# Inverse roots as exp(-ln/2) on ScalarE, and the last expert job's rows added on chip, in a one-core two-layer decoder trunk

## What is computed

```python
def rmsnorm(x, g):
    y = x32 * lax.rsqrt(jnp.mean(x32 * x32, axis=-1, keepdims=True) + EPS)
    return y * g
def moe_ffn(h, w_router, b_router, wg, wu, wd):
    logits = jnp.einsum('btd,de->bte', h, w_router) + b_router
    probs = jax.nn.softmax(logits, axis=-1)
    top_p, top_i = lax.top_k(probs, TOP_K)          # 2 of 8
    top_p = top_p / jnp.sum(top_p, axis=-1, keepdims=True)
    gates = jnp.sum(jax.nn.one_hot(top_i, N_EXPERTS) * top_p[..., None], axis=-2)
    y = 0
    for e in range(N_EXPERTS):
        y = y + gates[..., e:e + 1] * swiglu(h, wg[e], wu[e], wd[e])
    return y
# per layer (the same for both kinds):
    x = x + rmsnorm(mix, g_post_mix)                # mix: conv or attention, and memory attention
    h = rmsnorm(x, g_pre_ffn)
    x = x + rmsnorm(f, g_post_ffn)                  # f: dense SwiGLU (2816) or moe_ffn (8 x 1408)
```

## Time and profile before

| | |
|---|---|
| median of three runs | 1848.36 us (1845.27 to 1849.92) |
| profiled execution, its own time | 1845.7 us |
| its span | 1843.5 us |
| mean granted TensorE clock | 0.952 |
| TensorE matmul busy | 1675.3 us (91%) |
| VectorE, ScalarE, GpSimd busy | 955.3, 738.1, 533.9 us |
| DMA, mean over the span | 153 GB/s |

### The profile page before, as it was taken

How to read it: one execution, slowest core, us unless ns; L and a number is a source line. 1 busy time by engine, 2 the same in 40 slices (tenths; PEclk the granted TensorE clock), 3 DMA queues, 4 the chain that set the end, 5 groups by cost and what they waited for, 6 DMA issues and landing times.

```text
span 1843.5 us, 28946 instructions
## 1 busy us (share of the span) xinstructions
PE 1675.3 (91%) x11254; PEld 1522.8 (83%) x11254; DVE 955.3 (52%) x1145; ACT 738.1 (40%) x964; POOL 533.9 (29%) x326
## 2 busy tenths in 40 slices
PE   6898787899999997899898998899999999999991
PEld 5898677899999997899666586888898988989891
DVE  6796534211111002322486514877686776868764
ACT  6354443222222122221355222554454554545443
POOL 1001222255555343132000020252332524325242
PEclk8899888999999998899898999999999999999996
DMA  6623202144445332021533415399798796987934
GB/s 202 123 90 123 69 23 69 46 142 142 142 142 174 101 131 92 23 92 61 193 126 87 143 58 137 137 284 279 212 269 231 228 270 212 283 217 237 262 126 156
DMA packets 345379, 282.65 MB, mean 153 GB/s; under 512 B 9585, under 2 KB 309661, under 8 KB 345175
## 3 DMA queue, kind: packets, MB, share of 16 engines
q1 hardware_dynamic: 325619, 253.45, 46.9%
q10 hardware_dynamic: 16532, 16.57, 2.6%
q0 software_dynamic: 3168, 11.80, 2.2%
HBM read 247.40 MB, written 35.10 MB: 153 GB/s over the span
## 4 chain that ended last, share of the span: by engine, by line
PE 44%; issue 25%; DVE 12%; POOL 11%; ACT 4%; DMA 1%; SPq 1%; POOLq 0%; ACTq 0%; DVEq 0%
PE ps L2191 34%; POOL ea L841 9%; DVE cT L1518 2%; PE ps L2319 2%; POOL ea L843 1%; DVE wlo L1395 1%; PE ps L2153 1%; DVE rstd L1360 1%; PE ps L2143 1%; PE ps L2216 1%; DVE zc L1837 1%; PE ps L2329 1%; PE ps L2560 1%; PE ps L2509 1%; ACT zc L1166 1%
## 5 line engine op out<-in xcount | busy, mean ns | idle before, releaser
L2720 PE MATMUL ps<-ejx,ewh 128*128 128x384 f32 x1408 | 405.0, 361 | 8.6 <-DVE esg L2049 3.4
L2013 DVE TENSOR_TENSOR ewl<-eraw,ewh 128x2048 fp32r<-128x2048 f32 (+1 forms) x144 | 303.9, 2112 | 161.4 <-ACT ewh L1273 161.0
L1273 ACT ACTIVATE ewh<-eraw 128x2048 fp32r<-128x2048 f32 (+1 forms) x144 | 255.2, 1773 | 278.1 <-PE ps L2723 156.8
L2723 PE MATMUL ps<-ejx,ewl 128*128 128x192 f32 x1408 | 353.9, 251 | 0.0
L2191 PE MATMUL ps<-hh,whi 128*128 128x260 f32 x1504 | 316.7, 293 | 39.0 <-DVE hl L1751 27.5
L2191 PE MATMUL ps<-hl,whi 128*128 128x260 f32 x1504 | 309.3, 288 | 0.0
L2191 PE MATMUL ps<-hh,wlo 128*128 128x260 f32 x1504 | 309.1, 288 | 0.0
L841 POOL TENSOR_TENSOR ea<-eat,ea 128x128 fp32r<-128x128 f32 x88 | 180.3, 2049 | 381.0 <-ACT ea L1308 381.0
L2191 PEld LDWEIGHTS ps<-hh,whi 128*128 128x128 f32 x1504 | 241.0, 195 | 43.2 <-issue 30.0
L2720 PEld LDWEIGHTS ps<-ejx,ewh 128*128 128x128 f32 x1408 | 266.0, 189 | 12.6 <-issue 8.8
L2723 PEld LDWEIGHTS ps<-ejx,ewl 128*128 128x128 f32 x1408 | 270.8, 192 | 0.0
(11 more groups left out here) (401 smaller groups left out, 2619.2 us busy)
## 6 DMA issues: line engine op xcount, KB each, us to landing
eraw<-in_w_gate_e SPq DMA_DIRECT2D x88, 512.0 KB, 4.7
eraw<-in_w_up_e SPq DMA_DIRECT2D x88, 512.0 KB, 6.1
eraw<-in_w_down_e SPq DMA_DIRECT2D x64, 512.0 KB, 6.4
eraw<-in_w_down_e SPq DMA_DIRECT2D x48, 256.0 KB, 2.7
xs<-zero ACTq DMA_DIRECT2D x10, 1152.0 KB, 4.8
raw<-in_w_gate_d SPq DMA_DIRECT2D x22, 512.0 KB, 3.9
raw<-in_w_up_d SPq DMA_DIRECT2D x22, 512.0 KB, 5.1
raw<-in_w_down_d SPq DMA_DIRECT2D x16, 512.0 KB, 4.3
```

Source lines behind the costliest of these rows:

```text
L1273: e.activation(ewh[:, s, 0:n], eraw[:, u % RAW, 0:n], ACT.Copy).then_inc(ew_hi, 1)
L2013: e.tensor_tensor(ewl[:, s, 0:n], eraw[:, u % RAW, 0:n], ewh[:, s, 0:n].bitcast(F32), ALU.subtract)\
L2720: e.matmul(ps[:, q, 0:2 * C], ewh[:, s, o:o + P], ejx[:, k, :, :].rearrange("p h n -> p (h n)"), start=(k == 0), stop=(k == KD - 1), skip_ ...
L2723: ins = e.matmul(ps[:, q, C:2 * C], ewl[:, s, o:o + P], ejx[:, k, 0, :], start=False, stop=(k == KD - 1), skip_group_check=True)
```

## The change

It has two parts.

**Inverse roots.** At roots 1 to 5, at the layer norm and at the router's small norm, ScalarE's root becomes a logarithm and a second ScalarE instruction exp(-0.5 ln) on the same tile; VectorE's reciprocals (128 x 520, and a small one) go. The function tables are preloaded as one set that holds both, in place of the root's.

```diff
-                e.activation(halves(rstd[:, :]), ps[:, 4:6, 0:HALF], ACT.Sqrt, scale=1.0 / D, bias=eps[:, :])\
+                e.activation(halves(rstd[:, :]), ps[:, 4:6, 0:HALF], ACT.Ln, scale=1.0 / D, bias=eps[:, :])\
                  .then_inc(root_ready, 1)
+                e.wait_ge(root_ready, n + 1)
+                e.activation(rstd[:, :], rstd[:, :], ACT.Exp, scale=-0.5).then_inc(rstd_ready, 1)
...
-            e.preload_act_table(ACT.Sqrt)
+            e.preload_act_table_set("natural_log_exp_and_others")
...
             def inverse(n):
 
-                e.wait_ge(root_ready, n + 1)
-                e.reciprocal(rstd[:, :], rstd[:, :]).then_inc(rstd_ready, 1)
                 e.wait_ge(rstd_ready, n)
 
```

```diff
-            with e.Fori(0, nj) as j:
+            def row_back(i, s):
+
+                n = P if i < NT else B
+                e.indirect_dma_start(out=(fo[i][0:n, :], fs1[i][0:n, :])[s], out_offset=None, in_=ys,
+                                     in_offset=bass.IndirectOffsetOnAxis(ap=sle[0:n, s, i:i + 1], axis=0))\
+                 .then_inc(yr_in[i], 16)
...
+            for m in range(KE):
+                if m == 3:
+                    e.wait_ge(er_done, nj * 4)
+                    e.wait_ge(ys_out, nj * 32 + 16)
+                    e.wait_ge(xs_in, 160)
+                    e.wait_ge(last_ready, 1)
+                if m == KE - 1:
+                    e.wait_ge(eg_done, nj * (2 * KE))
+                rest(last, m)
+                if 3 <= m <= 6:
+                    row_back(m - 3, 0)
+                    row_back(m - 3, 1)
+            row_back(NT, 0)
+            row_back(NT, 1)
...
+            def early_sum(i):
+
+                n = P if i < NT else B
+                e.wait_ge(f_act, FA[f"one{i}"])
+                e.scalar_tensor_tensor(out=fo[i][0:n, :], in0=fs1[i][0:n, :], scalar=gme[0:n, 1, i:i + 1],
+                                       in1=fo[i][0:n, :], op0=ALU.mult, op1=ALU.add).then_inc(f_dve, 1)
+
+            def early_lo(i):
+
+                n = P if i < NT else B
+                e.wait_ge(f_act, FA[f"hi{i}"])
+                e.tensor_tensor(flo[i][0:n, :], fo[i][0:n, :], fhi[i][0:n, :].bitcast(F32),
+                                ALU.subtract).then_inc(f_dve, 1)
...
+                if part >= 6:
+                    for i in ((0, 1), (2, 3), (4,))[part - 6]:
+                        n = P if i < NT else B
+                        e.tensor_scalar(ohm[0:n, i, :], colf[0:n, 0:P], own_last[0:n, i:i + 1], None, ALU.is_equal)
+                        for h in range(2):
+                            ins = e.tensor_scalar(ohd[i][0:n, CB * h:CB * h + CB], colf[0:n, P:C], own_last[0:n, i:i + 1], None,
+                                                  ALU.is_equal)
+                if part == 8:
+                    ins.then_inc(last_ready, 1)
...
+                    if u == 9 or u == 10:
+                        early_one(u - 9)
+                    if u == KE:
+                        selection(last)
+                        early_one(2)
+                        e.preload_act_table(ACT.Sqrt)
                     if u == KE + 1:
-                        for c in range(4):
-                            rows_hi(c, j * 4 + (4 + c + 1))
+                        early_one(3)
+                    if u == KE + 2 or u == KE + 3:
+                        early_hi(2 * (u - KE - 2))
+                        early_hi(2 * (u - KE - 2) + 1)
+                    if u == KE + 4:
+                        early_one(4)
...
+            def add_rows(i, part):
+
+                n = P if i < NT else B
+                b = F_BANKS[i]
+                for k in range(4):
+                    c, h = k // 2, k % 2
+                    if i == 0:
+                        if part == 0:
+                            e.wait_ge(f_act, FA[f"y{k}"])
+                        else:
+                            e.wait_ge(f_dve, FD[f"y{k}"])
+                    ins = e.matmul(ps[0:n, b + h, :], sel[:, c, i * P:i * P + n], (eyh, eyl)[part][:, c, 512 * h:512 * h + 512],
+                                   start=False, stop=(part == 1 and c == 1), skip_group_check=True)
+                return ins
+
+            open_tile(0)
+            open_tile(1)
+            add_rows(0, 0)
+            add_rows(1, 0)
+            add_rows(0, 1).then_inc(f_pe, 1)
+            add_rows(1, 1).then_inc(f_pe, 1)
+            for i in range(2, NF):
+                if i == NT:
+                    e.wait_ge(f_dve, FD["w0"])
+                open_tile(i)
+                add_rows(i, 0)
+                add_rows(i, 1).then_inc(f_pe, 1)
```

Further edits: the tail goes through the tiles of 128 rows first and the tile of 8 rows last; in job 0 `result_rows`, `zero_rows` and the store are dropped, and `load_rows(2)` moves from step 7 to step 12; the last job's store of the job before moves from step 10 to step 9:

```diff
-                if u == 7:
+                if u == 12:
                     e.wait_ge(er_done, 4)
                     e.wait_ge(xs_in, 160)
                     load_rows(2)
-                if u == 10:
-                    e.wait_ge(ey_ready, 4)
-                    store_rows(0)
+            e.sem_inc(ys_out, 32)
...
+                    if u == 1 and first:
+                        e.sem_inc(ey_low, 2)
+                        e.sem_inc(ey_ready, 4)
+                    elif u == 1:
                         result_rows(j + 1, j * 32 + 16, j * 2 + 2)
-                    if u == KE + 1:
+                    if u == KE + 1 and not last:
                         for c in range(4):
                             rows_lo(c, j * 4 + (4 + c + 1))
...
-            with e.Fori(0, nj) as j:
+            def selection(j):
+
+                e.wait_ge(last_ready, 2)
+                for c in range(4):
+                    q = EB[eb_at(2 * KE + c)[0]]
+                    eb_wait(j, 2 * KE + c)
+                    if c == 3:
+                        for h in range(2):
+                            for i in range(NT + 1):
+                                n = P if i < NT else B
+                                e.matmul(ps[:, q, 256 + h:257 + h], (ohm[0:n, i, :], ohd[i][0:n, :])[h], gate_last[0:n, i:i + 1],
+                                         start=(i == 0), stop=(i == NT), skip_group_check=True)
+                    for i in ((0, 1, 2), (3, 4))[c % 2]:
+                        n = P if i < NT else B
+                        o = P * (i % 3)
+                        ins = e.transpose(ps[:, q, o:o + n], (ohm[0:n, i, :], ohd[i][0:n, :])[c // 2], ident[0:n, 0:n])
+                    ins.then_inc(er_done, 1)
```

More of the change, by code:

```diff
@@ L2054, in expert_dve @@
+            def expert_dve(j, first=False, last=False):
                 for u in range(PER_JOB):
@@ L2624, in _ @@
                           tmp[0:E, 0, i * P:i * P + (P if i < NT else B)]) for i in range(NT + 1)])
-            def zero_rows(c):
-                for h in range(2):
-                    ins = e.matmul(ps[:, 2 + c, 256 * h:256 * h + 256], ones[:, :], zero[:, 0:256], start=True, stop=True)
-                return ins
-            for c in range(3):
-                zero_rows(c)
             copied_out(e, TP_XT + 8)
```

304 lines of the change are left out of this document (197 added, 107 removed).

## The result

The changed kernel takes 1824.92 us (median of 4 runs, 1821.79 to 1827.86), the kernel before 1846.82 (4 runs, 1844.79 to 1849.92): a ratio of 0.9877, 95% interval 0.9861 to 0.9894. It is faster by 22 us where 36.7 were forecast, and its median lies 0.9 us above the upper end of the range (1824). The profiled execution took 1821.79 us, its span is 1820.0 against 1843.5.

A forecast was written before the change was run, and what follows sets the result against it. TensorE's matmuls fill 91% of the span, so only its waits can be won; -13.4 - 2.5 - 6.0 - 15.7 + 0.8 + 0.1 = -36.7 us gives 1809.0 profiled, 1811.7 median; 8-in-10 range 1801 to 1824.

The forecast's parts named there:

- Inverse roots: Roots 1 to 5 and layer norm: first multiplication starts 2.8 us earlier without the reciprocal; 13.4 us won in sum.
- GpSimd's turn at roots 1 and 3: GpSimd's low part is let in between VectorE's multiplications, so each of these roots wins only 1.3 us.
- TensorE's clock: Behind roots 2, 4 and 5 the shorter wait may keep the clock from falling: 2.5 us won, between 0 and 7.8.
- one of three possible places: Roots 2, 4 and 5 could each lose 2.6 us of work to low clock; the forecast took 2.5 in all.
- Job 0: First expert job: waits for VectorE, low clock behind and a late weight in job 1 go; 6.0 us won.
- The end: After the last job's matmuls: tail with small reciprocals for five tiles, ending at 1827.8; 15.7 us won.
- The last job: Added groups, scalings and gathers nearly fit into idle time; with the selection and its copies, 0.8 us lost.
- a step over is paid by the weights prepared ahead: Last job: where VectorE's added groups, about 0.3 to 1.1 us each, overrun a step, weights prepared ahead cover it.
- 2.8 us "by count": Last job's selection: 10 transposes and 10 matmuls of one column, in place of sixteen transposes of 1.95 us together.
- The gathers: Rival, last job: GpSimd falls behind through gathers beside VectorE's subtraction, TensorE stands 5 us: 1816.7; chance 0.20.
- The written-out job: Rival, last job: instructions run once may arrive later than a loop's; at twice the pace 1889.4; chance 0.04.

The follow-up runs named there:

- a_only: The kernel before with the inverse roots alone changed (logarithm and exponential): 1835.80 us, ratio 0.9937.
- gates_wait: Changed kernel; in the last job ScalarE's first scaling of gathered rows waits for VectorE's gates, no longer for the last one-hot: 1819.69 us, ratio 0.9855.
- spread: gates_wait with down steps between the selection's parts and ScalarE's first two scalings behind the selection's first copies: 1818.62 us, ratio 0.9845; last job 79.4.
- half_gathers: Changed kernel without the four second gathers of 128 rows, the first row added twice: 1828.50 us (one run); last job 88.3.
- warm_router: Changed kernel with six of the eight matmuls of zero rows put back before the router's last waits: 1826.53 us, ratio 0.9881.
- best: late_high and spread together: 1809.80 us, ratio 0.9790 to the kernel before.
- best_down: best with TensorE's wait for all low parts of the dense hidden tiles moved to the down projection's third weight chunk: 1802.74 us, ratio 0.9744.
- best_warm: best with all eight matmuls of zero rows put back: 1806.33 us, ratio 0.9778.
- best_all: best_down with the eight matmuls of zero rows back as in best_warm: 1800.07 us, ratio 0.9746.
- b_only: Changed kernel with root and reciprocal back at all places, so without the new inverse roots: 1840.56 us, ratio 0.9963.
- late_high: gates_wait with ScalarE's next weight tile at roots 1 and 3 moved behind the eight tiles of x: 1811.99 us, ratio 0.9816.

## Why the prediction was wrong

By its own steps:

- **Inverse roots**, -13.4 forecast. 2.8 for each root whose scaling waits alone, 2.4 at the layer norm and 1.3 at root 1 came out as 2.8, 2.4 and 1.1; root 3 gave 1.7. The working held, GpSimd's turn at roots 1 and 3 included.
- **TensorE's clock**, -2.5. The shorter wait saved about 0.9 us of low clock at root 2 (1.7 lost behind it in place of 2.6), and what the stages hold over the 2.8 of the wait itself (2.7 with the router's small root) gives 0.8 at root 4 and, in a_only, 0.7 at root 5: 2.4 in all. That this comes so near to a term that I took as one of three possible places is luck: it was saved in parts at all three. What the term left out is the clock elsewhere: 2.6 us in the dense layer behind a wait that was the same as before, and 1.4 in the router, of which 0.8 to 1.2 come from matmuls that the change removed and that I had costed at nothing. I named them only as work of VectorE, and did not ask what kept the clock up there.
- **Job 0**, -6.0: -6.3. The 0.9 counted as job 1's lies ahead of its first matmul, in the stage of job 0.
- **The end**, -15.7: -15.6. In its parts the first reciprocal came 0.4 us later than forecast, the five tiles took the 13.3 forecast, and the last store 2.2 in place of 2.5.
- **The last job**, +0.8: +11.2. This is the step that failed, at the words "a step over is paid by the weights prepared ahead". I compared the added operations of each engine with that engine's idle time, and asked of waits only whether GpSimd would be late. The change adds a wait of ScalarE for VectorE's last one-hot ahead of a weight that VectorE needs. It costs 3.5 us by itself (gates_wait); 1.4 is the wait that is left there, which went when spread moved the two scalings and split the selection together; and 2.4 are the selection's own time at full clock, over that of the transposes before (spread). The rest of the 11.2, 3.9 us, is put down to the low clock by subtraction; the granted clock was 0.50 for 9.3 us behind the wait, which would allow up to 4.7. The selection itself was mis-sized too: I had counted ten matmuls of one column as ten instructions where the trace has twenty, and my 2.8 us "by count" doesn't come out of the earlier trace rows, where twenty instructions at the mean of 0.12 make 2.4. Measured at full clock it is 4.2.
- **The rivals.** The gathers don't set the last job (half_gathers); the range reached past that rival's 1816.7, and the true cause was twice its size. Four gathers ran beside VectorE's subtraction of two SBUF inputs; two were held up, to 3.25 and 2.45 us, and two were not (0.96 and 1.04). The Trainium skill ("SBUF — State Buffer", "Who interferes with whom") says that such an instruction doesn't hold up a GpSimd instruction that only writes. If an indirect DMA's issue is one, the first two speak against that rule and the other two for it, so it stays open here. The same section's rule that the first to issue keeps the ports agrees with the 5.00 us at root 1. The written-out job was not slower as such: in spread the whole job takes 79.4 us against the loop's 77.7, selection included.

## What to carry to other kernels

When code is added to engines that feed each other, idle time per engine is not the test. Write down for every added wait what stands behind it in that engine's list and who needs it, and follow that until it leaves the loop; a wait for the last of several results is worth splitting when only an early one is used. And a matmul whose result nobody reads may still be holding the clock: before it goes, look at the granted clock of the stretch behind it.

## What was not expected of the hardware

- A matmul of one column with 128 x 128 weights in float32 is two entries of about 0.13 us each at the upper clock (1.25 and 1.36 us for ten entries in spread) and 0.22 to 0.24 at the lower. Ten entries of 40 columns took the same 1.26 us (warm_router), so the number of columns is not the price here. Twenty entries in a row, without a wait, were followed by the lower clock in two of five kernels (best, best_down; not in spread, best_warm, best_all).
- The same wait of 3.25 us of TensorE in the dense layer was followed by half the clock at once in the changed kernel and all others that keep GpSimd's early turn (a_only, b_only, gates_wait, spread and three more), about 1.0 us later in late_high, best and best_warm, and not in the kernel before. The wait of 2.28 us at root 2 was followed by 0.50 in all seven kernels with the new roots and GpSimd's early turn, and by 1.00 in all five with the late turn. So the length of the wait alone didn't decide; at these two places the outcome went with the order of work ahead of it, and what in that order decides isn't shown. At root 4, behind the same 2.28 us, even the five kernels with the late turn differ (1.00 in late_high, best_down and best_all, down to 0.50 in best and best_warm).
- VectorE's instructions follow each other without a gap in the records, and still GpSimd came in between two of them at each of roots 1 and 3.
